# A fused two-block kernel: query factor inside the exponential, a shorter reciprocal root, and half of the transposed-probability copies on ScalarE

## The chip, the cores and the metric

The kernel runs on one core of a Trainium2 chip. The metric is the time of one execution on the device in microseconds (us), taken for the slowest core; here there is only one. The engines are TensorE (PE, with its weight loads PEld), VectorE (DVE), ScalarE (ACT), GpSimd (POOL) and SyncE (SP, which issues most DMAs). Each runs its own program in order and meets the others through semaphores.

## The reference, cut to what matters

Two transformer blocks on 256 tokens of width 1024. The first has two attentions on one normalised input (a "latent" one with 16 heads and a "differential" one with 8), then an expert layer with 16 experts. The second block follows. The change touches the normalisations and the 16-head attention:

```
def _rms_norm(x, w):
    xf = x.astype(jnp.float32)
    y = xf * lax.rsqrt(jnp.mean(xf * xf, axis=-1, keepdims=True) + EPS)
    return (y * w.astype(jnp.float32)).astype(x.dtype)
...
    q = _rms_norm(q, mla_q_hnorm_w)
    k = _rms_norm(k, mla_k_hnorm_w)
    q = jnp.concatenate([q[..., :MLA_NOPE_DIM], _apply_rope(q[..., MLA_NOPE_DIM:], cos, sin)], axis=-1)
...
        s = jnp.einsum('bhqd,bhkd->bhqk', qb, k).astype(jnp.float32) * scale
        p = jax.nn.softmax(s, axis=-1)
        return jnp.einsum('bhqk,bhkd->bhqd', p.astype(v.dtype), v)
```

The reciprocal root of a query row is one number for each row and head, so it may multiply the row of q, or the row of scores after it.

## The kernel before, in words

The order of all work is written out by hand, one program for each engine, and everything below names lines of the profiled kernel.

**Stages.** From 0 to about 117 us PE multiplies the normalised input by the columns of `w_in` and of the low-rank weights, in tiles of 128 rows of weights: first `c`, then `dq`, `uq0`, `uq1`, `ukv0`, `ukv1`, `dk`, `dv`, later `gate_a`, `gate_b` and `out`. Each tile of weights is split into a high and a low part in a ring of three buffers `w_split`: ACT writes the high part (`high_parts`, L545), DVE the low part (`low_parts`, L930), and PE reads the high part twice (L1566) and then the low part (L1571). ACT may write a buffer again when PE is done with the tile three before it. Between those copies DVE does the norms. From about 117 to 175 us runs the first attention (8 differential heads), from about 170 to 259 us the second (16 heads). After that come the merge, the projection `out`, the router, the expert stage (307 to 1228 us, each expert 12 MB or so of weights from memory), and the second block to the end.

**The second attention** is a software pipeline over i = 0 to 18. In step i, PE does in this order: T(i), four transposes of the head's queries and keys (L1747); S(i-1), the scores of the head before (L1757), which go to the one PSUM bank 5; half tiles of `gate_b` in steps 1 to 13; PT(i-2), the transposes of the probabilities (L1771) into bank 6; PV(i-3), the product with the values (L1782). DVE in step i takes the maximum of the scores (L1220), multiplies it by minus 96^-0.5 (L1221), copies PT(i-2) from bank 6 to SBUF (L1226), multiplies the output of head i-3 by the gate and the reciprocal sum (L1242), and in even steps splits a low part (L930). ACT in step i copies T(i) (L707), splits a high part in steps 0, 2, 3, 5, 7, 9 (`gate_b`) and 11, 13, 15 (`out`), and takes the exponential of head i-1 out of bank 5, one ACTIVATE for each half of the tokens (L719). S(i) may overwrite bank 5 only when the exponential of head i-1 is done. In step 6 DVE also sums squares for the first attention's output (L1253), in step 7 it takes a root of them, after which POOL scales that output (L511, L512). After the last exponential ACT loads the sigmoid's table and does two sigmoids of the second gate (L731); DVE (L1238) waits for the first and POOL (L516) for both.

**Roots.** `roots` (L895 to L902) computes a reciprocal square root on DVE with a guess from the bits and three Newton rounds, in 13 small instructions of which each waits for the one before. It is called 12 times: five times for the input norms (2 columns), once each for the ranks (4), the 64 query and key factors, the 16 outputs, and four times for head norms (32, 32, 32 and 8).

**The expert stage** has eight slots of 2 MB. SP fills them as soon as they are free, then waits until PE has used one.

## Time and profile before

| | |
|---|---|
| Runs | 1583.15 us median of 3 (1581.08 to 1585.79) |
| The profiled execution | 1583.97 us, of which the span is 1582.2 us |
| Mean granted TensorE clock | 0.857 of full speed |
| PE busy | 1234.2 us (78%) |
| DVE busy | 535.7 us (34%), 945 instructions |
| ACT busy | 394.3 us (25%) |
| POOL busy | 30.9 us (2%) |
| DMA | 493.29 MB, mean 312 GB/s; 424 to 430 GB/s in the expert stage |
| Chain that ended last | PE 43%, DMA 37%, DVE 14%, ACT 3% |

The span is the time from the first to the last instruction that the profiler saw; the execution's own time has 1.8 us around it. The shares are means over stages that have different limits: the expert stage is DMA, the last 220 us are PE, and in the first 260 us PE, DVE and ACT hand work to each other.

### The profile page before, as it was taken

Reading aid. Unit: us, or ns where it says so; the run is one execution under the profiler, and the core shown is the slowest. Engines: PE = TensorE matmul, PEld = TensorE weight load, DVE = VectorE, ACT = ScalarE, POOL = GpSimd, SP = SyncE. Lnnn points to the kernel's source line nnn. Section 1 sums busy time; section 2 is a strip of 40 time slices with the busy share of each in tenths; the row PEclk is TensorE's granted clock in tenths of the full one; section 3 lists DMA queues with packets and bytes.
Section 4 is the critical chain, followed back from the end, with each engine's and each line's share of the span. In section 5 each row is a group of like instructions: output and inputs, shape, how many; then the busy total and the mean of one; then the engine's idle time right before and its main releaser. Section 6 shows DMA issues by size and latency. Waiting matters only on the chain.

```text
span 1582.2 us, 20257 instructions
## 1 busy us (share of the span) xinstructions
PE 1234.2 (78%) x8444; PEld 797.0 (50%) x8444; DVE 535.7 (34%) x945; ACT 394.3 (25%) x621; POOL 30.9 (2%) x44
## 2 busy tenths in 40 slices
PE   8988889877766666667767766776676988999996
PEld 8866677732332332332332332332232776899885
DVE  6999676510010010010010010010010767766545
ACT  5646544310000000000000000000000565465433
POOL 0000120100000000000000000000000000000000
PEclk9999998787778878877767778778768999999999
DMA  7552213599999999999999999999999533555540
GB/s 288 194 165 93 94 81 148 238 380 426 429 429 428 428 429 429 428 429 429 428 428 429 428 428 429 428 429 428 429 429 424 178 125 133 175 178 182 202 169 27
DMA packets 56299, 493.29 MB, mean 312 GB/s; under 512 B 6659, under 2 KB 7997, under 8 KB 31677
## 3 DMA queue, kind: packets, MB, share of 16 engines
q1 hardware_dynamic: 55308, 491.61, 76.2%
q10 hardware_dynamic: 944, 1.05, 0.2%
q8 instruction: 32, 0.52, 0.1%
q14 instruction: 15, 0.12, 0.0%
HBM read 491.59 MB, written 1.05 MB: 311 GB/s over the span
## 4 chain that ended last, share of the span: by engine, by line
PE 43%; DMA 37%; DVE 14%; ACT 3%; issue 2%; DVEq 0%; SPq 0%; ACTq 0%
DMA ring<-in_expert_w_down 17%; DMA arena<-in_expert_w_down 15%; PE ps L1566 10%; PE ps L1875 8%; PE ps L1610 6%; PE ps L1859 6%; PE ps L1571 5%; DVE w_split L930 3%; PE ps L1891 3%; DMA ring<-in_expert_w_up 2%; DMA ring<-in_expert_w_gate 2%; DVE xs L1344 1%; DMA ring<-in_w_in 1%; PE ps L1899 1%; DVE stat L1055 1%
## 5 line engine op out<-in xcount | busy, mean ns | idle before, releaser
L930 DVE TENSOR_TENSOR w_split<-ring,w_split 128x1024 fp32r<-128x1024 f32 (+3 forms) x178 | 201.0, 1142 | 94.7 <-ACT w_split L545 93.8
L545 ACT ACTIVATE w_split<-ring 128x1024 fp32r<-128x1024 f32 (+3 forms) x178 | 174.2, 988 | 203.8 <-PE ps L1571 151.2
L1875 PE MATMUL ps<-arena 128*32 128x512 f32 x1024 | 155.1, 753 | 59.7 <-DMA arena<-in_expert_w_up 59.2
L1875 PE MATMUL ps<-ring,arena 128*32 128x512 f32 x1024 | 153.2, 747 | 59.5 <-DMA ring<-in_expert_w_up 59.1
L1340 DVE TENSOR_TENSOR arena<-arena,ps 128x512 f32<-128x512 f32 x16 | 11.0, 687 | 428.4 <-PE ps L1875 428.4
L1344 DVE TENSOR_TENSOR xs<-ps,xs 128x512 f32<-128x512 f32 x64 | 39.8, 684 | 320.5 <-PE ps L1899 320.5
L1859 PE MATMUL ps<-onehot,xn_hi 128*128 128x32 f32 x256 | 93.6, 368 | 44.1 <-DVE onehot L1325 44.0
L1891 PE MATMUL ps<-arena 128*32 128x256 f32 x1024 | 85.5, 492 | 52.1 <-DMA arena<-in_expert_w_down 46.8
L1875 PEld LDWEIGHTS ps<-arena 128*32 128x32 f32 x1024 | 33.7, 128 | 173.1 <-DMA arena<-in_expert_w_up 93.5
L1875 PEld LDWEIGHTS ps<-ring,arena 128*32 128x32 f32 x1024 | 33.6, 129 | 171.1 <-DMA ring<-in_expert_w_up 89.7
L1891 PE MATMUL ps<-ring,arena 128*32 128x256 f32 x1024 | 79.1, 461 | 41.8 <-DMA ring<-in_expert_w_down 38.9
L1610 PE MATMUL ps<-hT_hi,w_split 128*128 128x256 f32 x608 | 110.3, 284 | 1.6 <-issue 0.8
L1859 PEld LDWEIGHTS ps<-onehot,xn_hi 128*128 128x128 f32 x256 | 82.3, 321 | 50.7 <-DVE onehot L1325 26.7
L1571 PE MATMUL ps<-w_split,hT_hi 128*128 128x512 f32 (+1 forms) x320 | 88.0, 388 | 14.0 <-DVE w_split L930 14.0
L1566 PE MATMUL ps<-w_split,hT_hi 128*128 128x512 f32 (+1 forms) x320 | 90.5, 395 | 8.3 <-DVE hT_lo L939 2.8
L1610 PEld LDWEIGHTS ps<-hT_hi,w_split 128*128 128x128 f32 x608 | 95.0, 192 | 2.1 <-issue 1.0
L1859 PE MATMUL ps<-onehot,xn_lo 128*128 128x32 f32 x256 | 93.6, 368 | 0.0
L1566 PE MATMUL ps<-w_split,hT_lo 128*128 128x512 f32 (+1 forms) x320 | 86.4, 383 | 0.0
L1891 PEld LDWEIGHTS ps<-arena 128*32 128x32 f32 x1024 | 37.3, 135 | 97.0 <-DMA arena<-in_expert_w_down 65.5
L1859 PEld LDWEIGHTS ps<-onehot,xn_lo 128*128 128x128 f32 x256 | 83.1, 325 | 0.0
L779 ACT ACTIVATE arena<-ps 128x512 f32<-128x512 f32 x16 | 9.6, 597 | 294.4 <-PE ps L1880 294.4
L1891 PEld LDWEIGHTS ps<-ring,arena 128*32 128x32 f32 x1024 | 37.1, 127 | 75.3 <-DMA ring<-in_expert_w_down 41.6
(331 smaller groups left out, 1517.2 us busy)
## 6 DMA issues: line engine op xcount, KB each, us to landing
arena<-in_expert_w_gate SPq DMA_DIRECT2D x32, 2048.0 KB, 36.0
ring<-in_expert_w_up SPq DMA_DIRECT2D x32, 2048.0 KB, 36.4
arena<-in_expert_w_down SPq DMA_DIRECT2D x32, 2048.0 KB, 29.6
ring<-in_expert_w_gate SPq DMA_DIRECT2D x32, 2048.0 KB, 36.0
arena<-in_expert_w_up SPq DMA_DIRECT2D x32, 2048.0 KB, 36.0
ring<-in_expert_w_down SPq DMA_DIRECT2D x32, 2048.0 KB, 30.0
ring<-in_w_ff SPq DMA_DIRECT2D x32, 1024.0 KB, 5.0
ring<-in_w_in SPq DMA_DIRECT2D x24, 1024.0 KB, 5.0
```

The costliest lines, as they stand in the source:

```text
L545: act.activation(w_split[:, n % WBUFS, 0, 0:cols], slot_view(slot, cols)[:, n % 2, :], ACT.Copy).then_inc(split_hi, 1)
L930: dve.tensor_tensor(buf[:, 1, :], w, buf[:, 0, :].bitcast(F32), ALU.subtract).then_inc(split_lo, 1)
L1055: dve.tensor_reduce(out, src, AX, ALU.add).then_inc(sq_read, 1)
L1340: dve.tensor_tensor(hid, hid_g, ps[:, 1, :], ALU.mult).then_inc(hid_ready, 1)
L1344: dve.tensor_tensor(xv, ps[:, 4 + j, :].rearrange("p (h d) -> p h d", h=HALVES), xv, ALU.add).then_inc(moe_added, 1)
L1566: pe.matmul(pset(SETS[name], h)[:, j * 512:j * 512 + width], left[part][:, kt, h * P:(h + 1) * P], w[:, 0, c0:c0 + width], start=first and ...
L1571: m = pe.matmul(pset(SETS[name], h)[:, j * 512:j * 512 + width], left[0][:, kt, h * P:(h + 1) * P], w[:, 1, c0:c0 + width], start=False, s ...
L1610: return pe.matmul(ps[:, SET[SETS[name]] + ct // 2, (ct % 2) * T:(ct % 2 + 1) * T], w[:, part_w, ct * P:(ct + 1) * P], left[:, kt, :], sta ...
L1859: m = pe.matmul(ps[:, 1, kt * CAP:(kt + 1) * CAP], src[:, h, kt * P:(kt + 1) * P], onehot[:, h, :], start=h == 0 and part == 0, stop=h == ...
L1875: m = pe.matmul(ps[j * CAP:(j + 1) * CAP, bank, :], xe[:, kt, :], w[:, r, j * FCOL:(j + 1) * FCOL], start=kt == 0, stop=kt == KT - 1, skip ...
L1891: m = pe.matmul(ps[j * CAP:(j + 1) * CAP, 3, 0:DCOL], hidT[:, r, c * CAP:(c + 1) * CAP], w[:, r, j * DCOL:(j + 1) * DCOL], start=c == 0 an ...
L1899: m = pe.matmul(ps[:, 4 + j, h * DCOL:(h + 1) * DCOL], scat[j * CAP:(j + 1) * CAP, h * P:(h + 1) * P], ye[j * CAP:(j + 1) * CAP, :], start ...
```

## The change

It has four parts.

1. The roots of the queries are multiplied by 96^-0.5 once (one small DVE instruction). The multiplication of all of q by them (L1145, 128x3072) goes. The exponential of the second attention gets its factor from `stat`, a column for each head and half, in place of a constant; the maximum is multiplied by minus that column.
2. `roots` is 10 instructions in place of 13: a multiplication by -0.5 in place of a shift and a subtraction, then one round of higher order and one Newton round. It needs a fourth scratch row.
3. In steps 3, 5, ..., 17 of the second attention ACT makes the copy of PT(i-2), DVE only in even steps. ACT's copy stands behind the copy of T(i) and ahead of the high part and of the exponential.
4. ACT's loop has one step more (17), in which it only copies PT(15), ahead of the sigmoids.

```
-            for i in range(HEADS + 1):
+            for i in range(HEADS + 2):
                 if i < HEADS:
                     u = DHEADS + i
                     act.wait_ge(hT_done, u + 1)
                     act.wait_ge(hS_done, u - 1)
                     act.activation(qkT[u % 2][0:QK, :], ps[0:QK, 4, :], ACT.Copy).then_inc(hT_evac, 1)
+                if i >= 2 and i % 2:
+                    u = DHEADS + i - 2
+                    act.wait_ge(hP_done, u + 1)
+                    act.wait_ge(hO_done, u - 1)
+                    act.activation(pt_sb[u % 2], ps[:, 6, :].rearrange("p (k t) -> p k t", k=2), ACT.Copy).then_inc(hP_evac, 1)
                 if i in gate_b_at:
                     high_parts("gate_b", gate_b_at[i], gate_b_at[i] + 1)
                 if i in (11, 13, 15):
                     high_parts("out", (i - 11) // 2, (i - 9) // 2)
...
-                if i >= 1:
+                if 1 <= i <= HEADS:
                     u = DHEADS + i - 1
                     act.wait_ge(max_ready, u + 1)
                     act.wait_ge(hP_done, u - 1)
                     for h in range(HALVES):
                         e = act.activation(scores[u % 2][:, h, :], ps[:, 5, h * T:(h + 1) * T], ACT.Exp,
-                                           bias=mxn[u % 2][:, h:h + 1], scale=QK ** -0.5, accum_out=sums[u % 2][:, h:h + 1])
+                                           bias=mxn[u % 2][:, h:h + 1], scale=rstd_q[:, h * HEADS + i - 1:h * HEADS + i],
+                                           accum_out=sums[u % 2][:, h:h + 1])
...
-                step(dve.tensor_scalar(a.bitcast(I32), v.bitcast(I32), 1, None, ALU.logical_shift_right))
-                step(dve.tensor_scalar(y.bitcast(I32), a.bitcast(I32), -1.0, RSQRT_MAGIC, ALU.mult, ALU.add))
-                step(dve.tensor_scalar(v, v, -0.5, None, ALU.mult))
-                for k in range(3):
-                    step(dve.tensor_tensor(a, y, y, ALU.mult))
-                    step(dve.tensor_tensor(a, a, v, ALU.mult))
-                    last = dve.scalar_tensor_tensor(out if k == 2 else y, a, 1.5, y, ALU.add, ALU.mult)
...
+                step(dve.tensor_scalar(y.bitcast(I32), v.bitcast(I32), -0.5, RSQRT_MAGIC, ALU.mult, ALU.add))
+                step(dve.tensor_tensor(a, y, y, ALU.mult))
+                step(dve.tensor_tensor(a, a, v, ALU.mult))
+                step(dve.tensor_scalar(b, a, 0.375, -1.25, ALU.mult, ALU.add))
+                step(dve.tensor_tensor(b, b, a, ALU.mult))
+                step(dve.scalar_tensor_tensor(y, b, 1.875, y, ALU.add, ALU.mult))
+                step(dve.tensor_tensor(a, y, y, ALU.mult))
+                step(dve.scalar_tensor_tensor(a, a, -0.5, v, ALU.mult, ALU.mult))
+                last = dve.scalar_tensor_tensor(out, a, 1.5, y, ALU.add, ALU.mult)
...
             roots(ss_h, rstd_h, 2 * n_heads, QK)
+            step(dve.tensor_scalar(rstd_q, rstd_q, QK ** -0.5, None, ALU.mult))
...
-            step(dve.tensor_tensor(qh, qh, rstd_q.unsqueeze(2).to_broadcast([P, n_heads, QK]), ALU.mult))
...
-                    dve.tensor_scalar(mxn[u % 2][:, 0:2], mxn[u % 2][:, 0:2], -QK ** -0.5, None, ALU.mult).then_inc(max_ready, 1)
+                    dve.scalar_tensor_tensor(mxn[u % 2][:, 0:2], mxn[u % 2][:, 0:2], -1.0, rstd_q[:, i - 1::HEADS], ALU.mult,
+                                             ALU.mult).then_inc(max_ready, 1)
...
-                    dve.wait_ge(hP_done, u + 1)
-                    dve.wait_ge(hO_done, u - 1)
-                    dve.tensor_copy(pt_sb[u % 2], ps[:, 6, :].rearrange("p (k t) -> p k t", k=2)).then_inc(hP_evac, 1)
+                    if i % 2 == 0:
+                        dve.wait_ge(hP_done, u + 1)
+                        dve.wait_ge(hO_done, u - 1)
+                        dve.tensor_copy(pt_sb[u % 2], ps[:, 6, :].rearrange("p (k t) -> p k t", k=2)).then_inc(hP_evac, 1)
```

**How the order moves.** On ACT, step 5 of the second attention and the copy of step 6, before. The 96x512 row is the copy of T, the `w_split` row the high part, the two 128x256 rows the exponential.

```order
L707 ACTIVATE arena<-ps 96x512 [waits hS_done,hT_done]
L545 ACTIVATE w_split<-ring 128x1024 [waits tile_used,dense_loaded2]
L719 ACTIVATE arena,stat<-ps,stat 128x256 [waits hP_done,max_ready]
L719 ACTIVATE arena,stat<-ps,stat 128x256
L707 ACTIVATE arena<-ps 96x512 [waits hS_done,hT_done]
```

The same place on ACT with the change (its lines are numbered a little higher):

```order
L709 ACTIVATE arena<-ps 96x512 [waits hS_done,hT_done]
L714 ACTIVATE arena<-ps 128x512 [waits hO_done,hP_done]
L547 ACTIVATE w_split<-ring 128x1024 [waits tile_used,dense_loaded2]
L726 ACTIVATE arena,stat<-ps,stat 128x256 [waits hP_done,max_ready]
L726 ACTIVATE arena,stat<-ps,stat 128x256
L709 ACTIVATE arena<-ps 96x512 [waits hS_done,hT_done]
```

The copy of PT, 128x512, now stands between the copy of T and the high part, so that both the high part and the exponential come behind its wait for `hP_done`.

On DVE, step 5 of the second attention, before: reciprocal, maximum, its factor, the copy of PT(3), and two instructions for the output of head 2.

```order
L1214 RECIPROCAL stat<-stat 128x2
L1220 TENSOR_REDUCE stat<-ps 128x2 [waits exp_done,hS_done,dve_step]
L1221 TENSOR_SCALAR stat<-stat 128x2 [waits dve_step]
L1226 COPY arena<-ps 128x512 [waits hO_done,hP_done]
L1242 SCALAR_TENSOR_TENSOR arena<-ps,stat,arena 128x64 [waits hO_done]
L1242 SCALAR_TENSOR_TENSOR arena<-ps,stat,arena 128x64
```

And with the change:

```order
L1225 RECIPROCAL stat<-stat 128x2
L1231 TENSOR_REDUCE stat<-ps 128x2 [waits exp_done,hS_done,dve_step]
L1232 SCALAR_TENSOR_TENSOR stat<-stat 128x2 [waits dve_step]
L1255 SCALAR_TENSOR_TENSOR arena<-ps,stat,arena 128x64 [waits hO_done]
L1255 SCALAR_TENSOR_TENSOR arena<-ps,stat,arena 128x64
```

The copy is gone from the odd step.

On ACT, the end of the second attention, before: the last exponential, the table load and the sigmoids of the second gate.

```order
L719 ACTIVATE arena,stat<-ps,stat 128x256 [waits hP_done,max_ready]
L719 ACTIVATE arena,stat<-ps,stat 128x256
L731 ACT_TABLE_LOAD
L731 ACTIVATE arena<-arena 128x2x512 [waits gate_in]
L731 ACTIVATE arena<-arena 128x2x512
```

And with the change:

```order
L726 ACTIVATE arena,stat<-ps,stat 128x256 [waits hP_done,max_ready]
L726 ACTIVATE arena,stat<-ps,stat 128x256
L714 ACTIVATE arena<-ps 128x512 [waits hO_done,hP_done]
L739 ACT_TABLE_LOAD
L739 ACTIVATE arena<-arena 128x2x512 [waits gate_in]
L739 ACTIVATE arena<-arena 128x2x512
```

The copy of PT(15) stands ahead of the table load, so that the load waits for PT(15) too.

## Rows read from the trace of the kernel before

**Rows 1.** Windows: bounds, length, busy PE, PEld, DVE, ACT, POOL, clock, DMA, GB/s.

```profile
216.00:220.00 4.00, 2.61 (x20) 2.28 (x19) 3.97 (x6) 2.25 (x6) 3.92 (x2) 1.00 0.46 197
248.00:252.00 4.00, 4.00 (x17) 3.52 (x17) 2.13 (x5) 1.29 (x5) 0.00 (x0) 0.50 0.00 0
304.00:308.00 4.00, 1.13 (x6) 1.09 (x6) 2.92 (x6) 0.00 (x0) 1.32 (x1) 0.65 0.00 0
```

**Rows 2.** Waits, 79 to 114 us: waiter <- releaser: total, times, longest.

```profile
PE ps L1571 <- DVE w_split L930: 4.3, 6, 1.5
```

**Rows 3.** Timeline, PE's waits for low parts: start, duration, instruction, idle before.

```profile
89.19 1.21 PE L1571 MATMUL ps<-w_split,hT_hi 128*128 128x512 f32 x4 [0.76 <-DVE w_split L930]
102.19 1.21 PE L1571 MATMUL ps<-w_split,hT_hi 128*128 128x512 f32 x4 [0.98 <-DVE w_split L930]
110.06 1.21 PE L1571 MATMUL ps<-w_split,hT_hi 128*128 128x512 f32 x4 [1.51 <-DVE w_split L930]
```

**Rows 4.** Timeline, 78 to 109 us, ACT and DVE.

```profile
78.92 1.90 ACT L579 ACTIVATE xn<-arena 128x2048 f32<-128x2048 f32 x1
80.98 2.28 DVE L1055 TENSOR_REDUCE stat<-xn 128x32 f32<-128x2048 f32 x1
105.39 3.35 DVE L1145 TENSOR_TENSOR arena<-arena,stat 128x3072 f32<-128x3072 f32 x1
```

**Rows 5.** Timeline and waits of the second block, 1255 to 1275 us, DVE's root.

```profile
1261.69 0.19 DVE L900 TENSOR_TENSOR stat<-stat 128x32 f32<-128x32 f32 x1
1261.92 0.19 DVE L901 TENSOR_TENSOR stat<-stat 128x32 f32<-128x32 f32 x1
PE ps L1571 <- DVE w_split L930: 4.0, 3, 1.6
```

**Rows 6.** Timeline of PE in steps 5, 6, 9 and 10 of the second attention.

```profile
199.54 1.03 PE L1757 MATMUL ps<-arena 96*128 96x256 f32 x4
201.79 0.60 PE L1771 MATMUL ps<-ident,arena 128*128 128x128 f32 x4
203.50 1.03 PE L1757 MATMUL ps<-arena 96*128 96x256 f32 x4
218.92 1.10 PE L1757 MATMUL ps<-arena 96*128 96x256 f32 x4 [1.39 <-ACT arena L719]
221.25 0.60 PE L1771 MATMUL ps<-ident,arena 128*128 128x128 f32 x4
224.19 1.10 PE L1757 MATMUL ps<-arena 96*128 96x256 f32 x4 [1.07 <-ACT arena L719]
```

**Rows 7.** Timeline of ACT and DVE in steps 5, 8 and 9.

```profile
199.74 0.59 ACT L707 ACTIVATE arena<-ps 96x512 f32<-96x512 f32 x1 [1.08 <-PE ps L1747]
200.23 1.05 ACT L545 ACTIVATE w_split<-ring 128x1024 fp32r<-128x1024 f32 x1
202.42 0.69 DVE L1226 COPY arena<-ps 128x512 f32<-128x512 f32 x1 [0.51 <-PE ps L1771]
215.83 0.69 DVE L1220 TENSOR_REDUCE stat<-ps 128x2 f32<-128x512 f32 x1
223.03 0.47 ACT L719 ACTIVATE arena<-ps,stat 128x256 f32<-128x256 f32 x1 [2.83 <-DVE stat L1221]
```

**Rows 8.** Two lines of ACT: durations min/median/max in ns, first and last start.

```profile
L677 ACT ACTIVATE arena<-ps,stat x8: 453/465/476, 115.1 to 159.0; 128x256 f32<-128x256 f32 x8
L678 ACT ACTIVATE arena<-ps x8: 364/374/385, 115.4 to 159.4; 128x256 f32<-128x256 f32 x8
```

**Rows 9.** Timeline, the end of the second attention.

```profile
251.73 1.28 ACT L731 ACT_TABLE_LOAD   x1
253.02 2.00 ACT L731 ACTIVATE arena<-arena 128x1024 f32<-128x1024 f32 x2
255.10 2.35 POOL L516 TENSOR_TENSOR arena<-arena 128x1024 f32<-128x1024 f32 x1 [29.71 <-ACT arena L731]
255.34 3.19 DVE L1238 TENSOR_TENSOR arena<-arena 128x1024 f32<-128x1024 f32 x1
```

More of the change, by code:

```diff
@@ L216, in hybrid_blocks @@
         ss_h, rstd_h = stat[:, 312:376], stat[:, 376:440]
+        rstd_q, rstd_k = rstd_h[:, 0:HALVES * HEADS], rstd_h[:, HALVES * HEADS:]
         mxn = [stat[:, 80 + 4 * i:84 + 4 * i] for i in range(2)]
@@ L230, in hybrid_blocks @@
         rstd_2 = stat[:, 632:634]
+        nw.append(stat[:, 136:200])
         posc = sb("posc", [P, HALVES, 3], I32)
@@ L892, in roots @@
             def roots(ss, out, n, dim, ready=None):
-                v, a, y = nw[0][:, 0:n], nw[1][:, 0:n], nw[2][:, 0:n]
+                v, a, y, b = nw[0][:, 0:n], nw[1][:, 0:n], nw[2][:, 0:n], nw[3][:, 0:n]
                 step(dve.tensor_scalar(v, ss, 1.0 / dim, EPS, ALU.mult, ALU.add))
-                step(dve.tensor_scalar(a.bitcast(I32), v.bitcast(I32), 1, None, ALU.logical_shift_right))
-                step(dve.tensor_scalar(y.bitcast(I32), a.bitcast(I32), -1.0, RSQRT_MAGIC, ALU.mult, ALU.add))
-                step(dve.tensor_scalar(v, v, -0.5, None, ALU.mult))
-                for k in range(3):
-                    step(dve.tensor_tensor(a, y, y, ALU.mult))
-                    step(dve.tensor_tensor(a, a, v, ALU.mult))
-                    last = dve.scalar_tensor_tensor(out if k == 2 else y, a, 1.5, y, ALU.add, ALU.mult)
-                    if k < 2 or ready is None:
-                        step(last)
-                last.then_inc(ready, 1) if ready is not None else None
+                step(dve.tensor_scalar(y.bitcast(I32), v.bitcast(I32), -0.5, RSQRT_MAGIC, ALU.mult, ALU.add))
[7 more added lines that the diff above has]
+                last = dve.scalar_tensor_tensor(out, a, 1.5, y, ALU.add, ALU.mult)
+                if ready is None:
+                    step(last)
+                else:
+                    last.then_inc(ready, 1)
             def square_half():
```

2 lines of the change are left out of this document (1 added, 1 removed).

## The prediction

> **What bounds the kernel now.** I read the page first, then the windows, the waits, and the timelines of the stretches that the change touches. The expert stage takes most of the time at the bandwidth of memory, and no edit is in it. Between prefetch and use the DMA engines stand still: from 304 to 308 us they move nothing [rows 1], since all eight slots are full and the first expert waits for the router. So what is gained or lost before 304 us moves the start of the expert stage, and the end, one for one. Four stretches are touched.
>
> In 79 to 114 us PE is nearly always busy, but six times it waits for DVE's low part, 4.3 us in all [rows 2]; three of these are 0.76, 0.98 and 1.51 us [rows 3]. DVE sets the end there and PE is close behind, so that what DVE saves is worth at most those 4.3 us. The first attention that follows is a chain through DVE; the change leaves it alone, and it simply starts earlier.
>
> In the second attention PE sets the pace in most steps: the scores of heads 4 and 5 start at 199.54 and 203.50, one step of 3.96 us, with no idle time before either [rows 6]. In steps 6 to 9 and 14 to 16 it waits for an exponential, which waits for DVE's maximum [rows 6, 7].
>
> In the second block DVE's root and the scaling behind it hold PE up three times, 4.0 us together [rows 5]. The other roots lie beside PE work. Behind them the chain of waits is almost all PE, and there a shorter DVE is worth nothing.
>
> **The roots and the scaling of q, 58 to 114 us.** Three instructions go from each call. In a dependent chain one costs 0.23 us from start to start (1261.69 to 1261.92) [rows 5], so a call is 0.69 us shorter; the call for the 64 factors gives 0.47, because one small multiplication of about 0.22 comes in. L1145 took 3.35 us [rows 4]. That is 0.69 + 0.47 + 0.69 + 3.35 = 5.2 us of DVE, of which PE can take this much. The first 0.69 (about 60 us) removes a small gap of some 0.3, but then DVE meets ACT: the squares of the keys start at 78.92 and take 1.90, and DVE's sum over them started at 80.98, only 0.1 us after they end [rows 4]. DVE keeps a lead of 0.1 there. The next root raises it to 0.55, and the gap of 0.76 gives PE another 0.25, up to 0.55. The third raises it to 1.24, and the gap of 0.98 gives 0.69. L1145 was the cause of the gap of 1.51 [rows 3], which goes whole. PE ends `dv` 0.3 + 0.25 + 0.69 + 1.51 = 2.75 us earlier; the rest of the 5.2 becomes idle time of DVE. I take -2.7. The ends are -1.5 (only the last gap) and -4.3 (all six). The calls before 40 us I count at nothing: DVE waits for PE or ACT behind both.
>
> **The copy on ACT, odd steps.** Follow step 5. PE starts the scores of head 4 at 199.54, the gate half tile, and PT(3) at 201.79; the next scores, of head 5, start at 203.50, that is 1.71 after PT(3) [rows 6]. They need the exponential of head 4. Before, that ran while PE was in the gate tile. Now ACT first waits for PT(3). A reader of PT starts 0.63 after it (DVE's copy, 202.42) [rows 6, 7]. ACT's copy has the size of L707, whose follower starts 0.49 after it (199.74 to 200.23); the high part, 1.05, overlaps its neighbour by the same 0.10 and takes 0.95 [rows 7]. So the exponential starts at PT + 0.63 + 0.49 + 0.95 = 2.07. From an exponential's start to the scores that it holds up it is 1.16 (223.03 to 224.19) [rows 6, 7]. The factor from memory adds to it: the same copy with a column as factor takes 465 ns, with a constant 374 [rows 8]; 0.09 for each ACTIVATE, 0.18 for the pair. The scores start at PT + 2.07 + 1.16 + 0.18 = 3.41 in place of 1.71: 1.70 us later. After a pause PT follows the scores by 2.33 (218.92 to 221.25) and not by 2.25 [rows 6], so 1.78 for each such step. The even step between has its exponential early and recovers nothing, for PE has no slack in it. Steps 3, 5, 11 and 13 are of this kind: 4 x 1.78 = +7.1.
>
> The Trainium skill, "ScalarE: Activation LUTs", section "What ACT_TABLE_LOAD costs", has about 93 ns for each operand taken from a column in an ACTIVATE, whatever its function. This speaks against the change, and by that rule the trace agrees with 91 ns, for a copy; no row here has an exponential with two columns.
>
> Steps 7 to 9: in step 7 the exponential waits for DVE's sum of squares anyway, so ACT's copy is hidden; +0.18. In step 8 DVE has lost its copy (0.6) and three steps of the root (0.6) ahead of the maximum of 215.83 [rows 7], -1.2, and +0.18. In step 9 ACT is last again: the scores follow PT(7) by 3.41 and PT(7) follows the scores of head 8 by 2.33, 5.74 against 5.27 before (218.92 to 224.19) [rows 6]: +0.5. Together -0.4. In step 15 DVE's two gate multiplications hide ACT's copy to within 0.1. The longer exponential adds 0.18 in steps 2, 14, 15 and 16, +0.7. The attention: 7.1 - 0.4 + 0.7 = +7.4. The ends: +5.5, if POOL holds DVE less in steps 7 to 9 and one of the four steps finds the maximum late anyway, and +9.
>
> **The end of the attention.** The table load began at 251.73, right behind the last exponential, the sigmoids at 253.02, each 1.0 long; POOL started at 255.10 and DVE's L1238 at 255.34 [rows 9]. Now the load stands behind the copy of PT(15), which follows the last exponential and runs at the lower clock, so that it is read near 253.0 on the old time scale (0.2 to the start of PT, twice 0.5 for its four transposes). Load and sigmoids come 1.9 later: the first ends at 255.9, the second at 256.9. L1238 starts 0.6 later but gets its 1.2 us before POOL, where now it takes 3.19 beside POOL [rows 9]; the last product waits for POOL, which ends near 259.4. I take +0.4, with -0.8 and +1.9 as the ends.
>
> The same section says that a switch of tables costs 2.66 us, of which 1.38 are a drain. By it POOL's part would come 1.4 later still. The row has 1.29 from the load's start to the sigmoid's [rows 9], so the measurement decides.
>
> **The second block.** 0.69 off the root, which lies on the path to the three waits of 4.0 us [rows 5]: -0.7, with 0 as the other end. The root for the router is done before the router's product, which is what the next step waits for: nothing.
>
> **The sum.** -2.7 + 7.4 + 0.4 - 0.7 = +4.4 us on the profiled execution's 1583.97: 1588.4. That execution was 0.8 above the median of the runs, 1583.15, so I forecast 1587.5.
>
> **Rivals.** *A free copy.* The exponential in odd steps is set by DVE, as it is in steps 7 and 15, and ACT's wait hides behind it. It decides where the factored maximum is ready later than PT + 2.07. For it: exponentials waited for DVE, that of head 8 for 2.83 us [rows 7]. Against it: in steps 5, 11 and 13 that wait ends before PT starts, with PE never idle [rows 6]. Then the second attention gains 1.2 from step 8 and pays the longer exponentials, about 0.7: 1583.15 - 2.7 - 0.7 - 0.5 = 1579.2.
>
> *The clock falls.* PE pauses 1.7 us in every second step. From 216 to 220 us it was busy 2.61 of 4 and kept the full clock; from 248 to 252, after two pauses, it had 0.50, which is 1.2 of 2.4 GHz [rows 1]. At the lower level two steps of 7.9 us PE work take 15.8 in place of 9.7. One such pair gives 1593.6. The first row speaks against it, yet the pause of step 13 comes close to those that cost the clock.
>
> *The front gives less.* DVE's lead is lost in further waits on ACT, and PE takes only the 1.51 behind L1145, and nothing in the second block: 1587.5 + 1.2 + 0.7 = 1589.4.
>
> **How the numbers follow.** The forecast 0.58, its own range 1585 to 1590; the free copy 0.17; the clock 0.12; the weaker front 0.13. A measurement of this kernel tells about 0.3% from no change, 4.7 us: below 1578.4 or above 1587.9. Faster: half of the free copy, 0.09. Slower: four tenths of the forecast (0.23), the clock (0.12) and nearly all of the weaker front (0.11), 0.46. Within: 0.45. The range 1579.5 to 1591.5 leaves out the lower part of the free copy and most of the clock.
>
> **What would show it.** In the profile after, the scores L1757 of heads 3, 5, 11 and 13 should start some 3.4 us after PT, with about 1.7 us of idle time released by the exponential, and the even ones without idle time. ACT's copy should start 0.6 after PT, the high part next, then the exponential, and what ACT waits for should be PE's L1771. The exponential should take 0.56 in place of 0.47. PE should wait for low parts about 1.5 us between 75 and 114 in place of 4.3, and `dv` should end near 114.4. The expert stage should start 4 to 6 us later and last as long. I am wrong if PE is never idle in steps 5, 11 and 13, if the first attention starts less than 1.5 us earlier, or if the expert stage changes its length.

## The result, and the profile after

The changed kernel takes 1593.25 us, median of 5 runs (1587.44 to 1597.63), against 1585.79 us for the kernel before in the same series (1581.08 to 1587.99). The ratio is 1.0043 [1.0026, 1.0059], some 6.8 us slower. A second series gave 1.0055 [1.0035, 1.0075]. The forecast was 1587.5 us with a range to 1591.5: the sign was right, the size was not.

The first profile taken of the changed kernel has a span of 1585.4 us, 3.2 above the span before. By it alone the forecast's +4.4 would look good, but it is of the fastest of the five runs. So I first read it for the mechanism, and then three more for the size. From here on DVE, ACT and PE lines are those of the changed kernel: L1770 (scores) and L1784 (transposes) were L1757 and L1771, L726 (exponential) was L719, L547 (high part) was L545, L1584 was L1571, L941 was L930.

Timeline of PE in steps 5, 6, 8, 9 and 10, which answers to [rows 6]:

```profile
200.10 1.03 PE L1770 MATMUL ps<-arena 96*128 96x256 f32 x4
202.34 0.60 PE L1784 MATMUL ps<-ident,arena 128*128 128x128 f32 x4
205.76 1.10 PE L1770 MATMUL ps<-arena 96*128 96x256 f32 x4 [1.54 <-ACT arena L726]
215.87 1.10 PE L1770 MATMUL ps<-arena 96*128 96x256 f32 x4 [1.95 <-ACT arena L726]
220.21 1.10 PE L1770 MATMUL ps<-arena 96*128 96x256 f32 x4
222.54 0.60 PE L1784 MATMUL ps<-ident,arena 128*128 128x128 f32 x4
225.95 1.10 PE L1770 MATMUL ps<-arena 96*128 96x256 f32 x4 [1.54 <-ACT arena L726]
```

Timeline of ACT in step 5, which answers to [rows 7]; L714 is the added copy:

```profile
200.30 0.59 ACT L709 ACTIVATE arena<-ps 96x512 f32<-96x512 f32 x1 [0.56 <-PE ps L1760]
202.98 0.60 ACT L714 ACTIVATE arena<-ps 128x512 f32<-128x512 f32 x1 [2.09 <-PE ps L1784]
203.47 1.05 ACT L547 ACTIVATE w_split<-ring 128x1024 fp32r<-128x1024 f32 x1
204.42 0.56 ACT L726 ACTIVATE arena<-ps,stat 128x256 f32<-128x256 f32 x1
205.50 0.58 ACT L709 ACTIVATE arena<-ps 96x512 f32<-96x512 f32 x1
```

The chain is the forecast one, link by link. ACT is idle 2.09 us until PT (202.34) is there, copies at PT + 0.64, starts the high part 0.49 later, the exponential 0.95 after that at PT + 2.08, and the scores start at 205.76, which is PT + 3.42 in place of 1.71. The same 3.41 or 3.42 stands in steps 3, 9, 11 and 13. The exponential itself takes 560 ns; the same group before had a median of 469. Here are all its instances of the second attention, durations min/median/max:

```profile
L726 ACT ACTIVATE arena<-ps,stat x32: 554/560/566, 180.8 to 257.5; 128x256 f32<-128x256 f32 x32
```

The Trainium skill, "ScalarE: Activation LUTs", section "What ACT_TABLE_LOAD costs", gives about 93 ns for an operand taken from a column: 469 to 560 is 91, now seen on an exponential that has two of them.

The front, waits of 75 to 112 us (the second row is the wait of [rows 2]) and the longest gaps left in the timeline, for [rows 3]:

```profile
PEld ps L1584 <- DVE w_split L941: 3.7, 5, 1.0
PE ps L1584 <- DVE w_split L941: 1.7, 4, 0.6
```

```profile
88.76 1.20 PE L1584 MATMUL ps<-w_split,hT_hi 128*128 128x512 f32 x4 [0.60 <-DVE w_split L941]
97.70 1.20 PE L1584 MATMUL ps<-w_split,hT_hi 128*128 128x512 f32 x4 [0.48 <-DVE w_split L941]
101.06 1.20 PE L1584 MATMUL ps<-w_split,hT_hi 128*128 128x512 f32 x4 [0.33 <-DVE w_split L941]
104.40 1.20 PE L1584 MATMUL ps<-w_split,hT_hi 128*128 128x512 f32 x4 [0.32 <-DVE w_split L941]
```

PE waits 1.7 us in place of 4.3, about the 1.5 that was forecast; the other three profiles of the changed kernel have 1.6 to 1.8. At the place of [rows 4], DVE's sum starts 81.07 and ACT's squares end 81.05: ACT is the limit there, as before.

```profile
79.14 1.91 ACT L581 ACTIVATE xn<-arena 128x2048 f32<-128x2048 f32 x1
81.07 2.29 DVE L1066 TENSOR_REDUCE stat<-xn 128x32 f32<-128x2048 f32 x1 [0.28 <-ACT xn L581]
```

The end of the attention, for [rows 9]. As forecast the table load stands behind the copy of PT(15), the first gate product has DVE for itself (1.22 in place of 3.19). The two additions behind it (L1275) do not wait for POOL; the first runs beside it and takes 2.87 us, the second 1.21:

```profile
259.34 0.60 ACT L714 ACTIVATE arena<-ps 128x512 f32<-128x512 f32 x1 [1.20 <-PE ps L1784]
259.96 1.28 ACT L739 ACT_TABLE_LOAD   x1
262.44 1.22 DVE L1251 TENSOR_TENSOR arena<-arena 128x1024 f32<-128x1024 f32 x1 [0.88 <-ACT arena L739]
263.33 2.54 POOL L518 TENSOR_TENSOR arena<-arena 128x1024 f32<-128x1024 f32 x1 [36.82 <-ACT arena L739]
264.09 4.00 DVE L1275 TENSOR_TENSOR arena<-arena 128x1024 f32<-128x1024 f32 x2
```

The second block, waits of 1253 to 1277 us, for [rows 5]. Two of the three waits are left, of 1.33 and 0.77 us. In the other three profiles of the changed kernel they are 1.33 and 1.65 us, so that the usual sum is 3.0 in place of 4.0:

```profile
PE ps L1584 <- DVE w_split L941: 2.1, 2, 1.3
```

What the first profile has beside this is one odd step. Timeline of PE, step 12:

```profile
235.65 2.00 PE L1770 MATMUL ps<-arena 96*128 96x256 f32 x4 [1.54 <-ACT arena L726]
237.09 1.42 PE L1579 MATMUL ps<-w_split,hT_hi 128*128 128x512 f32 x2
239.14 0.64 PE L1584 MATMUL ps<-w_split,hT_hi 128*128 128x512 f32 x2
```

Behind the pause of 1.54 us the scores take 2.00 us, where they take 1.10 behind the same pause in step 5. The granted clock from 236 to 240 us is 0.61. The step from head 11 to head 12 is 5.68 us in place of 4.04. This is the rival mechanism "the clock falls", at a smaller price than I had given it.

**Where the 6.8 us are.** The table has the mean length of each stage (rounded, one execution to a profile), from profiles of three executions of the kernel before and four of the changed one (spans 1582.2, 1587.5, 1587.1 against 1585.4, 1591.3, 1595.5, 1597.4). The stages are cut at starts of PE's instructions: the first transposes of the first attention, the scores of heads 0, 3, 13 and 15 of the second, the merge's transposes, the first gather, the last down product of the experts, the first and last narrow product of the second block.

| stage | before | after | difference | forecast |
|---|---|---|---|---|
| front | 115.2 | 111.0 | -4.3 | -2.7 |
| first attention, to head 0 | 59.6 | 59.5 | -0.1 | 0 |
| head 0 to head 3 | 25.0 | 28.7 | +3.7 | +2.0 |
| head 3 to head 13 | 44.7 | 50.9 | +6.2 | +4.9 |
| head 13 to head 15 | 7.5 | 9.4 | +1.9 | +0.4 |
| head 15 to merge | 11.0 | 12.5 | +1.5 | +0.6 |
| merge to experts | 48.0 | 48.2 | +0.2 | 0 |
| expert stage | 915.7 | 915.4 | -0.3 | 0 |
| second block, first half | 50.4 | 49.7 | -0.7 | -0.7 |
| second block, second half | 181.5 | 179.8 | -1.7 | 0 |
| rest | 126.9 | 127.3 | +0.4 | 0 |
| span | 1585.6 | 1592.4 | +6.8 | +4.4 |

The difference of the means, 6.8, agrees with the loss that the runs show. The front's -4.3 is -3.4 where the clock stays up: in two of the three profiles before and one of the four after the granted clock fell to 0.83 between 10 and 20 us and cost 2 us. The other excesses over the forecast are in the second attention, 1.7 + 1.3 + 1.5 + 0.9 = 5.4 us.

Windows of the slower executions show why: bounds, length, busy PE, PEld, DVE, ACT, POOL, clock, DMA, GB/s. First the third profile of the changed kernel, span 1595.5:

```profile
172.00:184.00 12.00, 8.09 (x29) 6.63 (x30) 3.07 (x4) 5.75 (x9) 0.00 (x0) 0.66 0.24 85
184.00:196.00 12.00, 11.44 (x48) 9.36 (x48) 4.93 (x7) 3.72 (x8) 3.78 (x2) 0.77 0.16 55
208.00:216.00 8.00, 6.60 (x31) 5.60 (x32) 2.76 (x7) 3.53 (x11) 0.00 (x0) 0.79 0.01 3
244.00:260.00 16.00, 13.34 (x72) 11.68 (x71) 9.90 (x23) 7.64 (x19) 0.00 (x0) 0.79 0.00 0
260.00:276.00 16.00, 13.71 (x59) 12.78 (x60) 10.38 (x19) 6.75 (x16) 2.55 (x1) 0.54 0.01 2
```

Then the third profile of the kernel before, span 1587.1, whose head 0 comes 5.6 us later and whose head 15 comes 6.7 us earlier:

```profile
172.00:184.00 12.00, 8.44 (x32) 6.51 (x33) 8.55 (x14) 6.44 (x11) 0.00 (x0) 0.74 0.39 132
184.00:196.00 12.00, 8.95 (x45) 7.52 (x44) 2.28 (x4) 6.11 (x14) 0.00 (x0) 0.83 0.00 0
208.00:216.00 8.00, 8.00 (x55) 7.20 (x54) 5.50 (x12) 4.18 (x11) 0.00 (x0) 1.00 0.02 3
244.00:260.00 16.00, 11.94 (x88) 10.69 (x86) 13.96 (x34) 9.18 (x23) 0.00 (x0) 0.99 0.01 2
260.00:276.00 16.00, 15.20 (x69) 13.02 (x70) 10.07 (x15) 5.20 (x11) 2.54 (x1) 0.79 0.59 228
```

Both kernels lose clock at 172 to 196 us, behind PE's two waits of 2.4 to 2.7 us, and the changed one loses more: head 0 to head 3 is 29.9 us less its pause of 1.78, against 26.4. It loses clock again at 208 to 216 and from 244 on, where the kernel before has 1.00 and 0.99.

### The profile page after: what moved, and what is told of

Same layout as the page of the kernel before. It is cut to its first block, busy times and chain, and to the rows that moved or that the text cites. A ratio compares the mean times of both kernels' runs of the same rounds, so it can differ in the third digit from the quotient of the medians.

```text
span 1585.4 us, 20221 instructions
## 1 busy us (share of the span) xinstructions
PE 1231.6 (78%) x8444; PEld 795.2 (50%) x8444; DVE 520.3 (33%) x901; ACT 401.1 (25%) x629; POOL 31.0 (2%) x44
## 4 chain that ended last, share of the span: by engine, by line
PE 42%; DMA 40%; DVE 11%; ACT 3%; issue 2%; DVEq 0%; SPq 0%; ACTq 0%
DMA ring<-in_expert_w_down 15%; DMA arena<-in_expert_w_down 15%; PE ps L1579 11%; PE ps L1888 7%; PE ps L1623 6%; PE ps L1584 6%; PE ps L1872 5%; PE ps L1904 2%; DMA arena<-in_expert_w_up 2%; DMA ring<-in_expert_w_up 2%; DMA arena<-in_expert_w_gate 2%; DMA ring<-in_expert_w_gate 2%; DVE w_split L941 2%; DVE xs L1357 1%; DMA ring<-in_w_in 1%
## 5 line engine op out<-in xcount | busy, mean ns | idle before, releaser
L941 DVE TENSOR_TENSOR w_split<-ring,w_split 128x1024 fp32r<-128x1024 f32 (+3 forms) x178 | 200.6, 1139 | 96.4 <-ACT w_split L547 95.4
L547 ACT ACTIVATE w_split<-ring 128x1024 fp32r<-128x1024 f32 (+3 forms) x178 | 174.2, 988 | 197.9 <-PE ps L1584 145.3
L1904 PE MATMUL ps<-arena 128*32 128x256 f32 x1024 | 87.0, 499 | 52.6 <-DMA arena<-in_expert_w_down 48.2
L1888 PEld LDWEIGHTS ps<-ring,arena 128*32 128x32 f32 x1024 | 33.1, 127 | 170.4 <-DMA ring<-in_expert_w_up 91.4
L1872 PEld LDWEIGHTS ps<-onehot,xn_hi 128*128 128x128 f32 x256 | 80.5, 314 | 50.4 <-DVE onehot L1338 26.4
L1584 PE MATMUL ps<-w_split,hT_hi 128*128 128x512 f32 (+1 forms) x320 | 87.9, 387 | 9.7 <-DVE w_split L941 9.7
L1623 PE MATMUL ps<-hT_lo,w_split 128*128 128x256 f32 x304 | 74.7, 283 | 0.0
## 6 DMA issues: line engine op xcount, KB each, us to landing
arena<-in_expert_w_down SPq DMA_DIRECT2D x32, 2048.0 KB, 29.8
```

The costliest lines, as they stand in the source:

```text
L547: act.activation(w_split[:, n % WBUFS, 0, 0:cols], slot_view(slot, cols)[:, n % 2, :], ACT.Copy).then_inc(split_hi, 1)
L941: dve.tensor_tensor(buf[:, 1, :], w, buf[:, 0, :].bitcast(F32), ALU.subtract).then_inc(split_lo, 1)
L1584: m = pe.matmul(pset(SETS[name], h)[:, j * 512:j * 512 + width], left[0][:, kt, h * P:(h + 1) * P], w[:, 1, c0:c0 + width], start=False, s ...
L1623: return pe.matmul(ps[:, SET[SETS[name]] + ct // 2, (ct % 2) * T:(ct % 2 + 1) * T], w[:, part_w, ct * P:(ct + 1) * P], left[:, kt, :], sta ...
L1872: m = pe.matmul(ps[:, 1, kt * CAP:(kt + 1) * CAP], src[:, h, kt * P:(kt + 1) * P], onehot[:, h, :], start=h == 0 and part == 0, stop=h == ...
L1888: m = pe.matmul(ps[j * CAP:(j + 1) * CAP, bank, :], xe[:, kt, :], w[:, r, j * FCOL:(j + 1) * FCOL], start=kt == 0, stop=kt == KT - 1, skip ...
```

## The experiments

Each timed kernel ran in up to 12 runs beside 17 to 30 of the kernel before, whose medians were 1585.4 to 1587.2. That is 2 to 4 us above the three runs I had at the time of the forecast. The series ran on different chips, so a ratio is always to the kernel before in the same series, and a difference between two ratios carries the intervals of both.

**The changed kernel again, and the copy by itself.** e2 takes the copies of the odd steps back to DVE:

```
-                if i >= 2 and i % 2:
-                    ... act.activation(pt_sb[u % 2], ps[:, 6, :] ..., ACT.Copy).then_inc(hP_evac, 1)
...
-                    if i % 2 == 0:
-                        dve.wait_ge(hP_done, u + 1)
+                    dve.wait_ge(hP_done, u + 1)
```

e3 is the kernel before with these same lines added, and the loop's one step more. e4 is the changed kernel with the five lines of ACT's copy behind `e.then_inc(exp_done, 1)`.

> The changed kernel once more, for the spread of its stages. The forecast's sum gave +4.4 us over the kernel before, the ratio measured so far is 1.0043 (+6.8 us). Theory A (the sum was mis-sized by 2 to 3 us somewhere, the same in every execution): ratio 1.003 to 1.006 again, and a profile of another execution shows the merge transposes 6 to 8 us later than before and the expert stage as long. Theory B (TensorE's clock falls in more of the pauses of other executions): the profiled stage 170 to 267 us differs between executions by 2 to 4 us, with a lower granted clock in the longer one. Theory C (the rest lies in stages that the change does not touch): the attention reads the same within 1 us, the expert stage or the second block is 2 to 4 us longer.

> The changed kernel with all sixteen transposed-probability copies on DVE again; the factor in the exponential and the shorter roots stay. Theory A: what is left is -2.7 us of the front (the trace after shows the first attention 3.0 us earlier), -0.7 of the second block's root, and +0.3 to +1 for exponentials 0.18 us longer a pair: -2.4 to -3.4 us against the kernel before, ratio 0.998, and the scores of the odd steps start 1.7 us behind PT without idle time. The copy then costs 7 to 10 us in all. Theory B (clock): the same, but the difference to the changed kernel is 9 to 11 us, more than the 7.4 of the pauses. Theory C (elsewhere): still 2 to 3 us of loss that the copy does not explain, ratio 1.000 or above.

> The kernel before with only the copies of the odd steps moved to ScalarE, in front of the exponential; scaling of q, constant factor and long roots stay. Theory A: four pauses of 1.7 us (no 0.18 of the longer exponential in them: scores at PT + 3.2), so +6.4, less 0.6 in steps 7 to 9, +0.4 at the end: +6 us, ratio 1.004. Theory B: +9 to +10, ratio 1.006. Theory C: +6 at most, and the other stages as before. If the copy were free: within 1 us.

> The changed kernel, and ScalarE's copy of the odd steps stands behind the exponential of the same step in its queue, not in front. Theory A (the cost is the place in the queue, not ScalarE's busy time): the exponential runs while PE is in the gate tile, as before, no idle time in steps 3, 5, 11, 13, and the time falls to that of the kernel with DVE's copies or 0.5 to 1 us below it (DVE has 0.6 less in steps 7 to 9): ratio to the kernel before 0.997 to 0.998. Rival (ScalarE's added 0.5 us in every second step costs by itself, or the next transposes of q and k wait for its queue): 2 us or more above that, ratio 1.000 or above.

Measured: e1 1.0055 [1.0035, 1.0075]; e2 0.9984 [0.9970, 0.9998]; e3 1.0053 [1.0032, 1.0074]; e4 0.9991 [0.9976, 1.0006].

The copy costs 1.0055/0.9984 = 1.0071, 11 us, in the changed kernel, and 8.4 us by itself. The forecast had 7.1 for its four pauses. The rest of the change gains 2.5 us, as the terms said. e1's profile is theory B of its expectation: head 0 to head 3 took 29.6 us where the first profile had 25.7. e4 settles what the cost is: ACT does the same work as in the changed kernel, only behind the exponential, and some 10 us are gone. Its PE has no pause in step 5, scores of heads 4 and 5:

```profile
197.78 1.03 PE L1770 MATMUL ps<-arena 96*128 96x256 f32 x4
201.74 1.03 PE L1770 MATMUL ps<-arena 96*128 96x256 f32 x4
```

So the price is the place in ACT's queue. That DVE is relieved of eight copies brings nothing that can be measured here: e4 is not faster than e2 (its ratio lies above the 0.997 to 0.998 expected, which its interval still holds). In e3 the exponential is short, and its scores start 3.24 us behind PT (205.77 to 209.01), 0.18 sooner than in the changed kernel, as expected. e3's profile has such a pause in each of steps 3, 5, 11 and 13 (1.36 us in step 5), and the steps behind them take 4.03 or 4.04 us, none of them 5.65, so that pauses of this kind do not always cost the clock.

**Small products in PE's waits.** The kernel holds such a helper, which multiplies the identity by itself into a bank that nobody reads. Bank 6 is free ahead of the scores of head 1:

```
             for i in range(HEADS + 3):
+                if i == 2:
+                    keep_clock(6, 14)
...
+                if i == 1:
+                    keep_clock(6, 14)
                 for k in gate_b_halves.get(i, ()):
                     pe.wait_ge(gate_in, 2)
```

e6 is this on the kernel before, e7 on the changed one, and e8 on e4, with `keep_clock(4, 12)` more ahead of the scores of head 15. e5 is a second profile of the kernel before.

> The kernel before once more, for a second profile. In the first profile the scores of head 0 and of head 3 of the second attention stood 22.0 us apart, with the full clock throughout; in four kernels with the change or parts of it 24.0 to 27.9 us (25.7, 29.6 and 25.2 less a pause of 1.7 in the three with the copy on ScalarE; 24.0 and 25.4 in the two without), with a granted clock of 0.5 in some of it. If the clock falls there in any kernel (B1: the first profile was a favoured one), this profile shows 23.5 us or more and a time near 1587. If only the changed front makes it fall (B2), it shows 22.0 again.

> The kernel before, with 14 small products of the identity on TensorE in each of the two waits of 2.2 and 2.5 us that stand between the scores of head 0 and of head 1; nothing else changed. Theory B (clock): they cost nothing, since PE waits there (14 x 0.133 = 1.9 us at the full clock), the granted clock stays at 1.00 from 170 to 190 us, and the slower executions lose their 2 to 5 us: median 1 to 3 us lower, ratio 0.998 to 0.9995. If the clock does not fall there before (B2), ratio 1.000.

> The changed kernel with the same 2 x 14 small products. Theory B: the scores of heads 0 and 3 come 25.7 less 2.0 = 23.7 us apart, and the time falls by 2 to 5 us; the ratio to the kernel before goes from 1.0055 to 1.003 or below, and to the filled kernel before it is 1.004 to 1.005: the copy's 7 to 8.5 us less the 3.4 of the roots and L1145. Rival (the loss beyond the forecast is in the pauses of steps 3 to 13 or later): the fillers bring under 1 us, ratio 1.005.

> The changed kernel with ScalarE's copy behind the exponential, the same 2 x 14 small products, and 12 more in the wait of 1.9 us before the scores of head 15, where the profiles show the clock at half until 262 us. Theory B: the second attention's first steps as in the first profile of before, the last three steps at the full clock, 2 to 3 us earlier at the merge: ratio 0.996 to 0.998. If the last steps are bound by the exponentials and DVE and not by PE, the third group brings nothing and the ratio is 0.998.

Measured: e5 1589.28 us, span 1587.5, head 0 to head 3 in 26.6 us; e6 0.9998 [0.9986, 1.0010]; e7 1.0029 [1.0017, 1.0041]; e8 0.9997 [0.9985, 1.0009].

e5 takes away a premise of mine: the full clock of the profile before, from head 0 to head 3, was a favoured execution. e7 has 4.2 us less than the changed kernel, e6 nothing that can be measured less than its own, where 1 to 3 us were expected. Head 0 to head 3 took 22.0 to 26.6 us before and, less the pause of 1.78, 23.9 to 28.2 after; with the products it takes 23.10 in e6, 23.05 in e7 and 23.09 in e8. With the products the spread of that stretch is gone, which puts it down to the clock. The price I had given the products was wrong: 14 take two passes each and 3.0 us, not 1.9, more than the waits hold, which is why e6 lies above the 22.0 of the first profile of the kernel before, which had the full clock. e8 shows the same with its 12 (scores of head 15 at 4.95 us behind head 14 in place of 4.3), and brought nothing over e4; 0.996 to 0.998 was expected. Its profile also has a step of 7.18 us from head 7 to head 8, where e4's has 4.35; the granted clock from 212 to 216 us is 0.50 there.

**The arithmetic of the chain, the parts alone.** e9 is e7 with `keep_clock(4, 10)` ahead of the transposes of q and k in steps 4, 6, 8, 10, 12 and 14. e10 is e7 with ACT's copy behind the high part, still ahead of the exponential. e11 is the kernel before with the new `roots` only, e12 with the query factor only (the three edits at L1145, L1221 and L720, and the small multiplication).

> The changed kernel with the 2 x 14 small products, and 10 more (1.33 us at the full clock) in each of steps 4, 6, 8, 10, 12 and 14 in front of the transposes of q and k, where PE would pause 1.5 us for the exponential right behind them. All three profiles of kernels with the copy in front of the exponential and the changed factor show one step with the clock at half (5.65 us in place of 4.04). Theory B (the pauses cost the clock): those steps are gone, the pauses are filled, and the time falls by 1.6 to 2.5 us below that of the kernel with 2 x 14, ratio to before 1.0015 to 1.002. Rival (the 1.6 us is chance, or the transposes come too late for ScalarE): same or slower, 1.003 or above.

> The changed kernel with the 2 x 14 small products, and ScalarE's copy stands behind the high part in odd steps, still in front of the exponential. This tests the arithmetic of the chain. Theory A (the exponential starts at PT + 0.63 + 0.49 = 1.12 in place of 2.07): the scores of heads 3, 5, 11 and 13 start at PT + 2.46, the pauses shrink from 1.54 to 0.6 us, step 9 is back at 5.3, and with less pause the clock stays up: 4 x 0.95 + 0.4 = 4.2 less, to 5.8 with the half-clock step gone: ratio to before 1.0000 (0.999 to 1.001). Rival (what counts is ScalarE's sum of work in the step, 0.5 more wherever it stands): as the kernel with 2 x 14, 1.003.

> The kernel before with only the shorter reciprocal roots. Forecast's terms: 1.24 us before the first attention and 0.7 in the second block, -1.9 in all, ratio 0.9988; 14 us of spread between executions from the clock stay. If DVE's lead is lost in waits on ScalarE: the front gives nothing, -0.7, ratio 0.9996.

> The kernel before with only the query factor in the exponential (scaling of q gone, one small multiplication more, factor from memory), copies on DVE, long roots. Forecast's terms: -1.5 us before the first attention (1.3 if the small multiplication shows), exponentials 0.18 longer a pair in steps 2, 6 to 9, 14 to 16, +0.7 to +1.2: -0.3 to -0.8, ratio 0.9995 to 0.9998. With the roots' part it should add to what both together gave, 0.9984.

Measured: e9 1.0032 [1.0017, 1.0047]; e10 0.9998 [0.9982, 1.0013]; e11 0.9973 [0.9961, 0.9984]; e12 0.9986 [0.9974, 0.9999].

e10 confirms the sum of links: 0.95 us of high part taken out ahead of the exponential shortens the wait from 1.54 to 0.59 us, scores at PT + 2.47:

```profile
200.31 0.60 PE L1788 MATMUL ps<-ident,arena 128*128 128x128 f32 x4
202.78 1.10 PE L1772 MATMUL ps<-arena 96*128 96x256 f32 x4 [0.59 <-ACT arena L726]
```

It gave 4.9 us against e7, 4.2 to 5.8 expected. One link did not follow: the step from head 8 to head 9, expected back at 5.3 us, took 6.39. e9 missed for the reason named: its products take more than the pause holds, and each such step is 6.24 us in place of 5.66. The half-clock step is gone from its profile, and the time is the same. e11 is the surprise: 4.3 us where the forecast's terms gave 1.9. e11 and e12 together would make 6.5 us, and e2, which is both, gave 2.5. The difference of 4.0 us is a little more than the three intervals allow together (about 3.5), so the parts do not simply add, or one of the numbers is off by more than its interval; which one is open.

**Is it chance, and the version without the loss.** e13 and e14 are the changed kernel, e15 the kernel before, for the stage table. e16 is e11 with ACT's copy behind the exponential.

> A third profile of the changed kernel. From the scores of head 0 to those of head 3 it took 25.7 and 29.6 us in the first two, 24.8 with the small products. Theory B (the clock's fall there is the missing 2 to 4 us): 27 us or more in the typical execution, near 1593 us in all, and one step of 5.65 us in place of 4.04 between heads 4 and 14. Rival (chance in single profiles): 25.7 or less, and the rest lies elsewhere.

> A fourth profile of the changed kernel, with the same expectations as the third: 27 us or more from head 0 to head 3 in at least one of the two by theory B, and the time of each profile follows that stretch and the other stretches at half clock; by the rival it does not.

> A third profile of the kernel before. From the scores of head 0 to those of head 3 it took 22.0 and 26.6 us so far (23.5 with the copy alone, less the pause, where the kernel is the same up to there; 23.1 with the small products). Theory B: 24 us or less as the typical case, the second profile being the slow end. Rival: 25 us or more here too, so that this stretch does not tell the kernels apart.

> The kernel before with the shorter roots, and in odd steps ScalarE's copy of the transposed probabilities behind the exponential; the scaling of q and the constant factor stay. The roots alone gave 0.9973. The copy behind the exponential takes nothing from PE in steps 3, 5, 11, 13 (seen: 3.95 us a step) and DVE gets 0.6 us ahead of the maximum of head 8: 0 to 0.6 us less than the roots alone, ratio 0.997. If ScalarE's added work shows elsewhere (sigmoids and table load behind the copy of PT(15)): 0.5 to 1 us more, 0.998.

Measured: e13 1597.44 us, head 0 to head 3 in 29.9 us; e14 1599.16 us, 29.8 us; e15 1588.88 us, 26.4 us; e16 1.0006 [0.9991, 1.0020].

By e15 the rival of my expectation was right: 26.4, and not under 24, is usual for the kernel before as well, so that this stretch tells the kernels apart by about 1.7 us beside the pause, and not by 4. The rest of the clock's cost is in the half-clock step (one in each of the four profiles of the changed kernel) and in the last heads, 9.3 and 10.3 us from head 13 to head 15 in e1, e13 and e14 against 7.5. Pauses of the copy are not needed for it: e8 and e12, which have none in steps 3, 5, 11 and 13, show a granted clock of 0.50 behind the wait of 1.95 us in front of head 7, and steps of 7.18 and 7.15 us. e16 missed. It stands 5.2 us above e11, the roots alone, and the two intervals allow about 2.9 by chance: here the copy behind the exponential does cost something, unlike in e4 against e2 (1.1 us, within noise). Its profile has no pause in steps 3, 5, 11 and 13; one step of 6.40 us (heads 8 to 9) stands in place of 4.58. The trace shows what stands behind that step. With its copy gone, DVE ends the root of the first attention's output earlier, and POOL, which waits for that root, starts 1.23 us behind the scores of head 7 where it starts 1.83 behind them in e11. So POOL's later instructions fall on other work of DVE: the low part takes 2.82 us where it takes 1.44 in e11, and the factor of the maximum (128x2) comes later and is held for 1.39 us, until POOL's instruction ends at 224.71:

```profile
221.50 3.21 POOL L513 TENSOR_TENSOR arena<-arena,row 128x1024 f32<-128x1024 f32 x1
223.34 1.39 DVE L1230 TENSOR_SCALAR stat<-stat 128x2 f32<-128x2 f32 x1
```

In e11 the same instruction takes 0.95 us, and away from POOL 0.17. e10 and e12 have the same hold of 1.39 us, in the same step, of 6.39 and 6.12 us. That is 1.8 of e16's 5.2 us; no experiment moved POOL's work, and the rest is open.

**Products that fit.** e17 is e9 with 10, 10 and 6 products in place of 14, 14 and 10. e18 is e11 with 10 and 10.

> The changed kernel with small products that fit the waits: 10 and 10 (2.2 us each, by 3.04 us for 14 in the profiles with fillers) in the two waits ahead of the scores of head 1, and 6 (1.3 us) in each of steps 4, 6, 8, 10, 12 and 14. Theory B (clock): 22.0 + 1.8 = 23.8 us from head 0 to head 3, 49.3 from head 3 to head 13 (no half-clock step), full clock until head 13, and what is left against the kernel before is the sum of the forecast, +3 to +4.4 us: ratio 1.002 to 1.003. Rival (the products delay other work, or the clock falls all the same): 1.003 to 1.0045.

> The kernel before with the shorter roots, and 10 and 10 small products in the two waits ahead of the scores of head 1. The roots alone gave 0.9973. From head 0 to head 3 22.1 us in place of 23.6 in the profile of the roots alone; ratio 0.996 to 0.998. If the roots' 0.9973 was partly chance (forecast's terms give 0.9988), 0.998 to 0.9985.

Measured: e17 1.0004 [0.9990, 1.0018]; e18 0.9963 [0.9948, 0.9978], median 1579.75 us.

Windows of e17, as above:

```profile
172.00:184.00 12.00, 11.54 (x76) 10.15 (x75) 4.19 (x7) 8.32 (x15) 0.00 (x0) 1.00 0.25 97
208.00:216.00 8.00, 7.44 (x48) 6.55 (x47) 7.40 (x21) 3.82 (x8) 0.99 (x1) 1.00 0.71 272
244.00:260.00 16.00, 11.66 (x80) 10.68 (x79) 11.89 (x27) 9.40 (x19) 0.69 (x1) 0.92 0.01 1
```

And one filled pause (L1641 are the products, L1764 the transposes of q and k, L1774 the scores):

```profile
201.70 1.56 PE L1641 MATMUL ps<-ident 128*128 128x128 f32 x12
203.10 0.60 PE L1764 MATMUL ps<-ident,arena 128*96 128x128 f32 x4
203.84 1.10 PE L1774 MATMUL ps<-arena 96*128 96x256 f32 x4
```

The pauses are all there (the step still takes 5.66 us), and the clock is at 1.00 to head 13. Head 0 to head 3 takes 23.92 us and head 3 to head 13 takes 49.30; 23.8 and 49.3 were expected. The time falls from 1.0055 to 1.0004, 8 us, by products whose result nobody reads. That shows that the clock was part of the loss. It is more than the 5.4 us of the table, but within the two intervals. The ratio missed its expectation of 1.002 to 1.003 on the good side: that sum stood against a kernel before with the full clock, and the kernel before loses some too. In e17's profile the expert stage starts at 311.7 us, in the three of the kernel before at 311.0 in the mean. e18 has the lowest ratio here: short roots and the filled waits, without the rest of the change. Its 1.6 us over the roots alone lie within the noise.

## Why the forecast was wrong

**The anchor.** 2.6 of the 5.75 us between 1587.5 and 1593.25 are the kernel before itself. I stood the sum on the median of three runs, 1583.15, and in this series the same kernel had 1585.79. The rest, 3.1 us, is 7.5 in place of 4.4.

**The copy on ACT, odd steps: right in every link.** "The scores start at PT + 2.07 + 1.16 + 0.18 = 3.41" and they do. At the full clock (e17) head 3 to head 13 costs 49.30 - 44.70 = +4.6, where the terms gave 4.9.

**The rival that the clock falls: the step that failed.** I wrote that the first row of [rows 1] speaks against it, since PE kept the full clock through 216 to 220 us with 2.61 of 4 busy, and gave it a chance of 0.12 as an alternative at the price of a whole pair of steps. That is the step that was wrong: the sum put the clock's cost beside the pauses at nothing. It is no alternative. It comes on top of the chain, in pieces of different size in the four profiles, in the mean 1.7 us ahead of head 3, 1.3 between heads 3 and 13 (the half-clock step, 1.6), 1.5 in the last two heads, 0.9 to the merge, 5.4 us together; the front's gain beyond the forecast hides part of it. One profile of one execution could not show this; the second row of [rows 1], 0.50 at 248 us behind two pauses, was the sign that it does fall.

**The front: too small.** -3.4 at the full clock in place of -2.7. The kernels with one part put 1.6 us on L1145 (1.5 forecast) and 1.6 to 1.9 on the roots (1.24 forecast), in the start of the first transposes of e12, e16 and e18 against 113.86 in the profile of before that had the full clock.

**The end of the attention.** Table load, POOL and DVE came in the order and with the durations forecast; +1.5 with the clock in it, where +0.6 was summed (0.4 and the longer exponential) with an end of 1.9. The two additions at the end did not wait for POOL as forecast; one ran beside it at 2.87 us. The row this part was read from was itself an unfavoured one: from head 15 to the merge the first profile of before took 12.6 us, at a granted clock of 0.50, and the other two 10.2.

**The second block.** The root gave its 0.7: the last down product to the first narrow one is 50.3 or 50.4 us in every profile with the long root and 49.6 to 49.8 in every one with the short root. Behind it the changed kernel is another 1.7 us shorter in the mean, which I had not forecast. In the first profiles the granted clock at 1308 to 1313 us differs there (products of 0.91 us in place of 0.73, behind the same wait of 1.6), and no edit stands in it. It is not shown to come of the change: with the same instructions of this block the stretch took 179.0 us in e4's profile and 182.5 in e2's.

**The expert stage** starts 9.2 us later in the mean (311.0 against 320.2), where 4 to 6 were forecast, and is as long as before (915.3 to 915.9 us), as expected.

## What to carry to other kernels

On an engine that serves a tight chain and side work, a new instruction that waits costs the delay of whatever stands behind it in the queue, and not its own duration: 0.5 us of copy cost 1.7 us a step ahead of the exponential and no pause in those steps behind it. Behind it is not always free either: e4 lost nothing that can be measured against e2, e16 lost 5.2 us against e11, of which its profile puts 1.8 on a step in which POOL's work fell on DVE's. Sum such a chain link by link, and then add the clock: a pause of 1.5 us on PE that repeats can have a second price, which one profile may not show. Take the spread from several profiles before calling the clock safe, and where PE must wait, fill the wait with products that fit into it.

## What the hardware showed that I had not expected

- The same kernel's same stretch took 22.0 us in one execution and 26.6 in another, with the granted clock at 1.00 behind a first wait of 2.24 us, or down to 0.50 (1.2 of 2.4 GHz) behind one of 2.42. With products in the wait it took 23.10, 23.05 (less the pause) and 23.09 in three kernels.
- A filler product of the identity, 128x128, takes two passes and 0.22 to 0.24 us, where I had counted 0.13: the instruction behind 28 passes starts 3.04 us after the first of them in e6, and behind 12 passes 1.40 us in e17.
- Behind two pauses of 1.54 us the same scores took 1.10 us in one step and 2.00 in another of one execution, so the clock does not follow from the last pause alone.
- An instruction of DVE on 128x2 numbers that takes 0.17 us elsewhere took 0.75 to 1.73 us in steps 3, 8 and 9 wherever POOL was at work on 128x1024 beside it, in each of the 20 profiles, and ended 0.01 to 0.03 us behind the end of POOL's instruction.
- A switch of tables between the exponential and the sigmoid was 1.29 us again, from the load to the first sigmoid (259.96 to 261.25).
